# The first four weight chunks are issued behind x, ahead of SP's vectors

## The reference

```
h    = rmsnorm(x, attn_norm)          # x / sqrt(mean(x*x) + eps), times a gain vector
proj = h @ w_in                       # (256 x 2048) @ (2048 x 5376)
...                                   # three kinds of attention, w_out, then w_up, conv, w_down
scale, shift, gate = silu(c) @ ada_w + ada_b     # second block: from two condition vectors
```

## Time and profile before

| what | us |
|---|---|
| median of three runs | 2570.73 |
| the profiled execution's own time | 2570.87 |
| its span, first to last instruction | 2569.1 |
| PE busy in the span | 2417.5 (94%) |
| DVE busy | 1676.4 (65%) |
| ACT busy | 1061.0 (41%) |

### The profile page before, as it was taken

The page is one execution under the profiler, slowest core; times in us unless marked ns, Lnnn a source line. Parts: engine busy times, 40 slices in busy tenths (PEclk is TensorE's granted clock), DMA queues, the critical chain, the costliest instruction groups (busy, mean ns, idle before and its releaser), DMA issues.

```text
span 2569.1 us, 33896 instructions
## 1 busy us (share of the span) xinstructions
PE 2417.5 (94%) x11316; PEld 2016.7 (78%) x11316; DVE 1676.4 (65%) x2395; ACT 1061.0 (41%) x1667; POOL 70.6 (3%) x110
## 2 busy tenths in 40 slices
PE   5899999989999999999997999999999799999998
PEld 4789867877877877777775888888788688889976
DVE  3667765558787787687775856658677643556644
ACT  3556564445545555533343222222321443434333
POOL 0011210000000000000000000000000000000000
PEclk9899956999999999999998999999999899999999
DMA  8777700556666676677772645546565343512244
GB/s 184 223 253 232 227 1 1 156 153 207 221 225 208 218 225 210 205 250 249 236 247 82 201 147 174 160 148 192 181 202 185 105 132 101 156 58 73 65 136 139
DMA packets 229370, 434.47 MB, mean 169 GB/s; under 512 B 13680, under 2 KB 63720, under 8 KB 227721
## 3 DMA queue, kind: packets, MB, share of 16 engines
q1 hardware_dynamic: 223592, 419.00, 51.7%
q10 hardware_dynamic: 5376, 13.95, 2.4%
q0 software_dynamic: 288, 0.11, 0.0%
HBM read 426.16 MB, written 6.85 MB: 169 GB/s over the span
## 4 chain that ended last, share of the span: by engine, by line
PE 61%; issue 18%; DMA 8%; DVE 7%; ACT 4%; SPq 1%; DVEq 0%; POOL 0%; ACTq 0%; POOLq 0%
PE ps L507 44%; PE ps L517 9%; DMA raw<-in_w_down 4%; DMA raw<-in_w_in 4%; DVE lo L455 3%; ACT hi L451 2%; DVE ada_acc L484 2%; PE ps L538 1%; DVE ustage L1402 1%; PE ps L1875 1%; PE ps L1749 1%; PE ps L612 1%; PE ps L1737 1%; PE ps L1748 1%; PE ps L1755 1%
## 5 line engine op out<-in xcount | busy, mean ns | idle before, releaser
L451 ACT ACTIVATE hi<-raw 128x1024 fp32r<-128x1024 f32 x616 | 647.0, 1059 | 1179.4 <-PE ps L507 624.0
L455 DVE TENSOR_TENSOR lo<-raw,hi 128x1024 fp32r<-128x1024 f32 x616 | 744.9, 1223 | 556.9 <-ACT hi L451 553.1
L507 PE MATMUL ps<-hi,h_hi 128*128 128x512 f32 (+1 forms) x1472 | 581.0, 395 | 38.9 <-DVE lo L455 29.7
L507 PE MATMUL ps<-lo,h_hi 128*128 128x512 f32 (+1 forms) x1472 | 573.8, 390 | 0.0
L507 PE MATMUL ps<-hi,h_lo 128*128 128x512 f32 (+1 forms) x1472 | 573.5, 390 | 0.0
L484 DVE SCALAR_TENSOR_TENSOR ada_acc<-raw,csil,ada_acc 128x512 f32<-128x512 f32 x720 | 491.2, 748 | 7.4 <-DMA raw<-in_ada_w 7.2
L507 PEld LDWEIGHTS ps<-hi,h_hi 128*128 128x128 f32 x1472 | 280.0, 190 | 103.4 <-DVE lo L455 28.0
L507 PEld LDWEIGHTS ps<-hi,h_lo 128*128 128x128 f32 x1472 | 279.8, 190 | 54.7
L507 PEld LDWEIGHTS ps<-lo,h_hi 128*128 128x128 f32 x1472 | 280.2, 190 | 51.8
L507 PE MATMUL ps<-hi,g_hi 128*128 128x512 f32 x352 | 141.1, 401 | 5.7 <-DVE lo L455 5.6
L507 PE MATMUL ps<-hi,g_lo 128*128 128x512 f32 x352 | 139.2, 396 | 0.0
(11 more groups left out here) (281 smaller groups left out, 3137.0 us busy)
## 6 DMA issues: line engine op xcount, KB each, us to landing
raw<-in_ada_w SPq DMA_DIRECT2D x192, 512.0 KB, 4.3
raw<-in_w_up SPq DMA_DIRECT2D x176, 512.0 KB, 4.5
raw<-in_w_down SPq DMA_DIRECT2D x88, 512.0 KB, 5.4
raw<-in_w_in SPq DMA_DIRECT2D x96, 448.0 KB, 4.5
raw<-in_pool_w_in SPq DMA_DIRECT2D x64, 512.0 KB, 4.0
raw<-in_mla_w_in SPq DMA_DIRECT2D x56, 448.0 KB, 3.7
raw<-in_w_out SPq DMA_DIRECT2D x32, 512.0 KB, 4.8
raw<-in_pool_w_out SPq DMA_DIRECT2D x32, 512.0 KB, 4.7
```

The costliest lines, as they stand in the source:

```text
L451: act.activation(hi[:, slot, :, :], raw[:, slot, :, :], ACT.Copy).then_inc(hi_split, 1 + ada)
L455: dve.tensor_tensor(lo[:, slot, :, :], raw[:, slot, :, :], hi[:, slot, :, :].bitcast(F32), ALU.subtract).then_inc(lo_split, 1)
L507: mm = pe.matmul(ps[:, bank, 0:width], a[:, kt0 + k, tok * P:(tok + 1) * P], w[:, slot, k, 0:width], start=first and k == 0 and s == 0, st ...
```

## The change

SP issues the first four chunks of `w_in` directly behind x, and the ten vectors of its queue behind them. The same transfers are issued, with the same sizes and on the same queue. The loop that issued the four chunks before skips them (`skip=RING`); chunk 4 and all later ones are issued where they were.

```diff
             for i in range(TT):
                 sp.dma_start(xres[:, i, :], t["x"][0, i * P:(i + 1) * P, :]).then_inc(x_loaded[i], 16)
+            for c in range(RING):
+                load_chunk(sp, c, c, t["w_in"][0][c * CK_T * P:(c + 1) * CK_T * P, 0:W_IN], W_IN)
             sp.wait_ge(vecs_cleared, 1)
             for (tile, row), n, src in VECS[SP_VECS]:
...
-            def load_turn(first, i, order, weights, ada=None):
+            def load_turn(first, i, order, weights, ada=None, skip=0):
 
                 for at, (of_ada, m) in enumerate(order):
+                    if at < skip:
+                        continue
...
-            def first_panels(i):
-                load_turn(C_IN, i, IN_ORDER, lambda j: ..., (0, i * W))
-
-            first_panels(0)
+            def first_panels(i, skip=0):
+                load_turn(C_IN, i, IN_ORDER, lambda j: ..., (0, i * W), skip)
+
+            first_panels(0, RING)
```

More of the change, by code:

```diff
@@ L797, in rows @@
                 return w[j * CK_T * P:(j + 1) * CK_T * P, bass.ds(col0, width)], width
-            def first_panels(i):
-                load_turn(C_IN, i, IN_ORDER, lambda j: rows(t["w_in"][0], j % CH, (i * IN_PANELS + j // CH) * W_IN, W_IN), (0, i * W))
-            first_panels(0)
+            def first_panels(i, skip=0):
+                load_turn(C_IN, i, IN_ORDER, lambda j: rows(t["w_in"][0], j % CH, (i * IN_PANELS + j // CH) * W_IN, W_IN), (0, i * W), skip)
+            first_panels(0, RING)
             sp.wait_ge(bias_stored, 2 * 16)
```

## The result

The changed kernel takes 2570.77 us (median of 17 runs, 2567.22 to 2577.62), the kernel before 2565.32 (17 runs beside them, 2559.94 to 2571.04). The ratio is 1.0019, with a 95% interval of 1.001 to 1.0027: 2.6 to 6.9 us longer, a small but real loss, in the direction forecast and inside 0.3%. The profiled execution has a span of 2573.2 us against 2569.1.

A forecast was written before the change was run, and what follows sets the result against it. The prediction took the start to be bound by PE's wait for vectors, not weights. Later vectors gave +2.5 us, all else 0; on the median of 2570.73 that made 2573.2 us, range 2564 to 2579.

The forecast's parts named there:

- Who is waited for: At the start PE waits for vectors at 15.45; weights have 4.7 us of slack, so earlier weights are worth 0.
- Whose vectors are last before the change: The gate at 15.36 is q10's convolution vectors, issued by ACT; SP's vectors had some 4 us of slack.
- SP's issues cost nothing and end at 7.6: SP ends all fourteen issues at the same 7.6; its next work waits until 21.82, so its time costs nothing.
- The weights gain 1.5 us and land at 15.9: On q1 the fourth chunk lands at about 15.9 instead of 17.4, by 1.5 us; worth 0.
- SP's vectors land at 17.9, bounds 15.9 to 20.1: SP's vectors, behind 1.8 MB of weights on q1, move the gate by +2.5 us, bounds +0.5 to +4.7.
- the tail behind the last chunk: Small packets at the end of q1 use the engines badly, adding 0.5 us to 17.4.
- The convolution vectors slip too, by about one microsecond: On q10 they are through by about 16.5; cost 0 while SP's vectors are later, 1.1 us otherwise.
- Everything behind slides, nothing is absorbed: All work behind the gate, including the transfer-bound 30 to 90 us, slides by the same +2.5 us.
- The unmoved gate: Rival: the gate stays within half a microsecond, at most +0.5 us, time 2571; chance 0.20.
- the shortened start: Rival: earlier weights shorten the wait of `hi` of chunk 0 by up to 1.5 us, time 2569.2; chance 0.05.
- the collision: Rival: chunk 4's issue falls into ACT's second bias issue and waits 8.25 us, time 2581.5; chance 0.07.
- The clock did fall elsewhere: Rival: the shift puts other waits beside a fall of PE's granted clock, time 2565.3; clock or run luck downwards 0.10.

The follow-up runs named there:

- the second profile: The changed kernel run once more, unaltered, for another profile: gate 18.60 (+3.15), span 2570.6 us against 2569.1 for the kernel before.
- two chunks ahead: The changed kernel, but only chunks 0 and 1 issued ahead of SP's vectors: ratio 1.001 against the kernel before, +2.6 us.
- seven kernels: The changed kernel and six variants of it or the kernel before, all moving the gate (-2.27 to +7.58 us): times -2.3 to +8.7 us against the kernel before.
- the early kernel: The kernel before, with ACT's convolution vectors directly behind ident, stick and sinks last: ratio 0.9991, -2.3 us.
- the changed one with ACT's vectors early: The changed kernel, with ACT's convolution vectors directly behind ident, stick and sinks last: ratio 1.0 (0.9988 to 1.0011) against the kernel before.

## Why the prediction was right, and where its numbers were off

The mechanism held; that the forecast time of 2573.2 us lies only 2.4 above the measured 2570.77 is partly luck. Its base, the median of three runs, was 2570.73, and 17 runs give 2565.32: 5.4 us too high. The change was taken too small, +2.5 for +4.9 (2.6 to 6.9). The two errors offset each other.

- *Who is waited for.* Right. The weights had slack and the vectors none to speak of: the chunk issues moved by four microseconds bought nothing, and the early vectors 2.3 us at the gate (in time 2.3 too, but 0 to 4.6).
- *Whose vectors are last before the change.* Right, by reading which queue still moved small packets. Moving q10's convolution vectors took the gate from 15.45 to 13.18.
- *SP's issues cost nothing and end at 7.6.* The cost is right, the time wrong: 9.47. Issues behind four queued chunks take longer, up to 1.28 us each. It stayed covered, since the vectors had to wait for the chunks anyway.
- *The weights gain 1.5 us and land at 15.9.* Wrong: 17.35, no gain. The room at 8.6 to 9.9 was used (0.27 against 0.08 MB). That at 10 to 11 was not: q1 moved 0.18 MB, where 0.31 was taken, against 0.16 before. From 12 to 15.4 q1 then moved 0.10 MB less than before, of which more rows on q10 are 0.04. It cost the sum nothing because the weights' landing had the value 0; but the lower bound of the gate, 15.9, was set by it and was looser than it looked.
- *SP's vectors land at 17.9, bounds 15.9 to 20.1.* 18.31 and 18.51 in two profiles: +2.95 and +3.15, against +2.5. That all packets are through when they were before is right (17.0 in both). The mis-sized term is the tail behind the last chunk, 0.5 us in the sum and 0.96 measured (18.31 - 17.35). The sum put it down to small packets that use the engines badly; what the traces show is that the count comes late, 1.3 us behind the last packet, and 1.5 in the second profile. Before it was 0.5.
- *The convolution vectors slip too, by about one microsecond.* Right, q10's last packets pass before 16.2; and the count can come later still (16.73 with two chunks ahead, though q10 was empty at 15.5).
- *Everything behind slides, nothing is absorbed.* Right on the average of seven kernels, slope 1.03 plus or minus about 0.3; single profiles stray from it by up to 5 us at the 65th `hi`. In the two profiles of the changed kernel 0.6 to 1.3 us are added by the 65th `hi`. Gate and this together make 3.7 to 4.2, inside the measured 2.6 to 6.9. How much of the 4.9 in the middle is more than chance stays open.
- *The rivals.* The unmoved gate, the shortened start and the collision did not come: chunk 4's issue took 0.40 us, in its old place between ACT's two. The clock did fall elsewhere: the mean granted clock of 30 to 90 us is 0.78 against 0.86. But the early kernel has 0.78 there as well and is shorter in the median, and PE waits for chunks in that stretch at either level. From 90 to 100 us it is different: PE is busy for 9.4 of 10 us, and the granted clock is 0.76 in the changed kernel (0.74 in its second profile) against 0.98. So this rival is not excluded as a part of what the changed kernel loses beyond the gate. One profile of the kernel before cannot say whether its 0.98 is the rule.

## What to carry to other kernels

Before moving a transfer forward, ask who waits for it, and who waits for what it overtakes: small vectors that gate everything belong ahead of bulk data with slack. Rank queued transfers by the slack of their first user, and look per window at which queue still carries small packets, since a shared count names only the last issue. Where a large write competes with streamed weights, try it in pieces that each still have many source partitions, and spread the pieces over a stretch in which the DMA engines have room.

## What the runs showed of the hardware that was not expected

- A queue that was filled four microseconds earlier delivered hardly earlier: the first chunk landed at 13.1 against 13.6, the fourth at 17.35 against 17.4.
- Small transfers were counted as landed well behind their last packet: 0.5 us in the kernel before, 1.3 in the changed one, and 1.9 in the changed one with ACT's vectors early, with no packet of any queue under way in that time. Why the count comes so late is not shown.
- SP's small issues behind four chunk issues took up to 1.28 us against 0.57 at most.
- 84 us lost or 16 us gained with the same 4.7 MB, by the cut of the pieces: four partitions by 128 rows, or 8 and 16 partitions by 16 rows.
